# Rotary rows of the keys: a fold on TensorE for each head in the bank of its other rows, in place of one fold and a GpSimd copy

## The chip, the cores and the metric

The kernel runs on one core of a Trainium2 chip. The metric is the device time of one execution in microseconds, the median of several runs. A core has TensorE (PE in the profile, its weight loads PEld), VectorE (DVE), ScalarE (ACT), GpSimd (POOL) and SyncE (SP), which issues the loads from memory.

## What is computed

A network of two layers on 256 tokens of width 1024. Layer 0 mixes latent attention with a state-space scan (S5), layer 1 is a long convolution; each is followed by a mixture of 64 experts. All of the change lies in the keys of layer 0's attention, which the reference makes like this (cut):

```python
def mla_keys_values(part, kv_norm, w_ukv, k_qk, cos, sin):
    B, L, _ = part.shape
    c_kv = rmsnorm(part[..., :KV_LORA], kv_norm)
    kv = (c_kv @ w_ukv).reshape(B, L, MLA_HEADS, QK_NOPE + V_HEAD)
    k_r = jnp.broadcast_to(part[..., None, KV_LORA:KV_LORA + QK_ROPE], (B, L, MLA_HEADS, QK_ROPE))
    k = rmsnorm(jnp.concatenate([kv[..., :QK_NOPE], k_r], axis=-1), k_qk)
    if cos is not None:
        k = rope_tail(k, cos, sin)
    return k, kv[..., QK_NOPE:]
```

There are 8 heads. A key has 96 features: 64 of its own head (QK_NOPE) and 32 rotary ones (QK_ROPE), which are the same for all heads. They are made for 512 tokens, 256 of the sequence and 256 of the context.

## The kernel before

Everything lies in one arena of on-chip memory and in eight banks (`ps`, 128 rows x 512 f32), and each engine runs a program of its own; the order is written out by hand, and semaphores carry the dependences. `Chain.then` makes an engine wait for its own instruction. `mm` (L752) is TensorE's helper for a product, so nearly all products have that line; `f` (L1416) is ScalarE's.

The stage around the change goes as follows on TensorE. It projects the tokens: the latent of keys and values (`kvl`, bank 0), the rotary rows, the latent of the queries, and then the four parts of the S5 input (`proj_u`). Between these stand chunks of the modulation matrix (`ada_chunk`, L446: eight products with 24 columns each, four side by side in four quarters of bank 7), whose weights SyncE loads one after another, each when the one before has been used. The rotary rows have only 32 output rows, so their eight partial products are spread over the four quarters of bank 1 (group `g = k % 4`), and ScalarE copies the whole bank to `krl`. `fold` is a 128x32 matrix made of four 32x32 identities: a product with it adds up the four quarters. Before the change this product is made once (L851), into rows 64 to 95 of bank 1; ScalarE copies them to rows 64 to 95 of `krl` (L1467), and GpSimd, once all projections have been read, copies them to rows 64 to 95 of all eight heads of `kh` (L687, 32 x 4096).

After the projections come the S5 tables turned for each block (`b_piece`, L805), the queries' heads (L867 and on, 96 rows), and the keys' heads (L876 to L880): for each head a product of 64 columns of `w_ukv` with `kvl`, into rows 0 to 63 of bank `h % 3`. ScalarE evicts each to `kh[0:NOPE, h]` (L1492), and TensorE may run three heads ahead. After the eighth eviction TensorE goes on with S5 products (`estimates`, 64 columns each) and with the sums of squares of the queries' heads (`head_sum`, 32 columns each, heads in the order 0, 2, 1, 3, 4, 6, 5, 7, two in each quarter of bank 0; head 4 and later ones write rows 64 to 127). Then the values, `chunk_kernels` (L752, 32 columns), two idle products, and the scaling of the queries (`over_features`), which waits for VectorE's copies of the chunk kernels (L1854 to L1857).

VectorE meanwhile computes the S5 tables (L1790 to L1826), and between them the norms of the latents: L1838 and L1839 scale `kvl`. ScalarE squares `kh` for the norms of the keys from `square_head(4)` on, and waits for `kr_copied` before it (L1515). From there on the norms of the keys, the rotation (`rope`), the scores and the rest follow, each released by the one before; later loads of SyncE wait for `ada_used`, `ada_mm`, `y_mm`, `att_mm` and `x_mixed`, all of them signals of the computing engines.

Of the kernel before, what the change touches and what calls it, by code (L numbers as in the profile page):

```python
# [11 lines left out]
ACT = mybir.ActivationFunctionType  # L12
AX = mybir.AxisListType

P = 128
D = 1024
KD = D // P
L = 256
EPS = 1e-6
HEADS, NOPE, ROPE, VH = 8, 64, 32, 64  # L20
QKH = NOPE + ROPE
# [104 lines left out]
def program(nc, A):  # L126
# [8 lines left out]
    with ExitStack() as ctx:  # L135
        sems = {}

        def sem(name):
            if name not in sems:
                sems[name] = ctx.enter_context(nc.semaphore(name))  # L140
            return sems[name]
# [3 lines left out]
        ps = ctx.enter_context(nc.psum_tensor("ps", [P, 8, 512], F32))  # L145
# [11 lines left out]
        def at(a, width, rows=P):  # L157
            return ar[0:rows, a:a + width]
# [9 lines left out]
        def cst(name, rows=P):  # L168
            a, w = CST[name]
            return at(r_cst + a, w, rows)  # L170
# [4 lines left out]
        def tiles(a, k, n, rows=P):  # L175
            return at(a, k * n, rows).rearrange("p (k t) -> p k t", k=k)
# [27 lines left out]
        kh = tiles(ra, HEADS, 2 * L, QKH)  # L204
# [23 lines left out]
        w_ukv = at(rg + 1536, 1024)  # L228
# [3 lines left out]
        kvl, krl, ql = at(rk, 512), at(rk + 512, 512), tiles(rk + 1024, 2, L)  # L232
# [136 lines left out]
        def most_tokens(li, eng):  # L369
            return eng.value_load(flags[:, li:li + 1], min_val=0, max_val=L + HALF)  # L370

        def overflow(eng, body, most, s=1):

            with eng.If(most > s * S):
                with eng.Fori(0, NE) as i:
                    body(s, i)
                if s < L // S:
                    overflow(eng, body, most, s + 1)
            eng.nop()
# [295 lines left out]
        @block.gpsimd  # L675
        def _(pool):
            ch = Chain(pool, sem("pool_chain"), sem)
            ch.then(pool.memset(ones, 1.0), "ones_ready")
            pads = at(r_pad, 1)
            ch(pool.memset(pick2, 0.0))  # L680
            ch.then(pool.memset(pick2[:, 1:2], 1.0), "ones_ready")
            A8, B8 = tiles(tmp5, 2, NT5), tiles(tmp5 + 64, 2, NT5)
            t1, t2 = tiles(tmp5 + 128, 2, NT5), tiles(tmp5 + 192, 2, NT5)
            tt = pool.tensor_tensor
            pool.wait_ge(sem("kvl_evicted"), 4)
            pool.wait_ge(sem("proj_mm"), 8)
            ch.then(pool.tensor_copy(kh[NOPE:QKH], krl[NOPE:QKH].unsqueeze(1).broadcast_to([ROPE, HEADS, 2 * L])), "kr_copied")  # L687

            def squared(out_a, out_b, a, b):

                ch(tt(t1, a, a, ALU.mult))
                ch(tt(t2, b, b, ALU.mult))
                ch(tt(tmp_a, a, b, ALU.mult))
                ch(tt(out_b, tmp_a, tmp_a, ALU.add))
                ch(tt(out_a, t1, t2, ALU.subtract))

            def step(out, a, b, state, flipped, add, w1, w2):

                ch(tt(w1, a, state, ALU.mult))
                ch(tt(w2, b, flipped, ALU.mult))  # L700
                ch(tt(w1, w1, add, ALU.add))
                ch(tt(out, w1, w2, ALU.add))

            pool.wait_ge(sem("est_ready"), 8)
            a8, b8 = (v.unsqueeze(1).broadcast_to([P, XCH // 2, 2, NT5]) for v in (A8, B8))
            step(tree, a8, b8, est[:, 0:XCH:2], est[:, 0:XCH:2, ::-1], est[:, 1:XCH:2], wide, tree)
            squared(pair_a, pair_b, A8, B8)
            a, b, src, n = pair_a, pair_b, tree, 16
            for out in (est[:, 0:8], tree[:, 0:4], est[:, 0:2], st[:, 2:3]):
                n //= 2  # L710
                w1, w2 = wide[:, 0:n], wide[:, 8:8 + n]
                step(out, a.unsqueeze(1).broadcast_to([P, n, 2, NT5]), b.unsqueeze(1).broadcast_to([P, n, 2, NT5]),
                     src[:, 0:2 * n:2], src[:, 0:2 * n:2, ::-1], src[:, 1:2 * n:2], w1, w2)
                if n > 1:
                    squared(step_a, step_b, a, b)
                    a, b = step_a, step_b
                src = out
            pool.wait_ge(sem("combined"), 1)
            for j in range(XCH // 2 - 1):
                step(st[:, 4 + 2 * j], pair_a, pair_b, st[:, 2 + 2 * j], st[:, 2 + 2 * j, ::-1], pair_in[:, j], t1, t2)  # L720
            ch.then(pool.memset(pads, 0.0), "scan_done")

            pool.wait_ge(sem("combined"), 2)
            ch.then(pool.tensor_copy(stb, st[:, 1 + XCH:1:-1].rearrange("p s r (g d) -> p s r g d", d=2)[:, :, :, :, 1]), "scan_done")

            def moe_pool(li):
                ov_pad = at(r_pad + 1 - li, 1)

                def gather(out, index, name):
                    pool.indirect_dma_start(out, None, scr["h_scr"], bass.IndirectOffsetOnAxis(index, 0), bounds_check=L - 1,  # L730
                                            oob_is_err=False).then_inc(sem(name), 16)

                pool.wait_ge(sem("hscr_out"), 16 * (li + 1))
                pool.wait_ge(sem("tables_ready"), TABLES * (li + 1))
                pool.wait_ge(sem("tx_mm"), (li + 1) * NG)

                def more(s, i):
                    pool.wait_ge(sem(f"ov_d{li}"), i * OVD + OVD * NE * (s - 1) + OV_INDEX)
                    pool.wait_ge(sem(f"ov_t{li}"), i + NE * (s - 1) + 1)
                    pool.tensor_tensor(ov_pad, ones[:, 0:1], ones[:, 0:1], ALU.add).then_inc(sem(f"ov_t{li}"), 1)  # L740
                    gather(rows_of[0:S, 0], ib[:, 0:1], f"ov_q{li}")
                pool.memset(ov_pad, 0.0).then_inc(sem(f"ov_t{li}"), 1)  # L742
                overflow(pool, more, most_tokens(li, pool))

            moe_pool(0)
            moe_pool(1)
# [3 lines left out]
        def _(pe):  # L750
            def mm(out, lhsT, rhs, start, stop, skip=False):
                return pe.matmul(out, lhsT, rhs, start=start, stop=stop, skip_group_check=skip)  # L752
# [91 lines left out]
            def proj_u(i):  # L844
                for k in range(KD):
                    last = mm(ps[:, 3 + i, :], w_in[:, k, UOFF + i * P:UOFF + (i + 1) * P], hT[:, k], k == 0, k == KD - 1)
                last.then_inc(sem("proj_mm"), 1)
            pe.wait_ge(sem("uw_in"), 48)
            proj_u(0)
            pe.wait_ge(sem("kvl_evicted"), 2)  # L850
            mm(ps[NOPE:QKH, 1, :], cst("fold"), krl, True, True).then_inc(sem("proj_mm"), 1)  # L851
            ada_chunk(pe, FIRST + 1)
            proj_u(1)
            ada_chunk(pe, FIRST + 2)
            pe.wait_ge(sem("squared"), 4)
            pe.wait_ge(sem("kvl_evicted"), 4)
            for i in range(2):
                last = mm(ps[:, 2, 0:L], ones, sql[0][:, i * L:(i + 1) * L], i == 0, i == 1)
            last.then_inc(sem("norm_mm"), 1)
# [17 lines left out]
            for h in range(HEADS):  # L877
                if h >= 3:
                    pe.wait_ge(sem("kh_evicted"), h - 2)
                mm(ps[0:NOPE, h % 3, :], w_ukv[:, h * P:h * P + NOPE], kvl, True, True).then_inc(sem("head_mm"), 1)  # L880

            def estimates(b):
                q, r = b // 2, b % 2
# [528 lines left out]
        def _(act):  # L1412
            ch = Chain(act, sem("act_chain"), sem)

            def f(out, in_, func, **kw):
                return act.activation(out, in_, func, **kw)  # L1416
# [36 lines left out]
            ch.then(f(sql[1], kvl, ACT.Square), "squared")  # L1453

            def u_evict(i):
                act.wait_ge(sem("proj_mm"), 4 + min(i, 1) + i)
                ch.then(f(u_sb[:, i], ps[:, 3 + i, :].rearrange("p (c t) -> p t c", t=T5), ACT.Copy), "u_evicted")

            def b_evict(n):
# [3 lines left out]
                act.wait_ge(sem("bt_turned"), n + 1)  # L1463
                ch.then(f(bm[:, q % 2, 4 * hb:4 * hb + 4, r], ps[:, 1 + n % 2 if n >= 8 else 2 * (n % 2), :].rearrange("p (t m) -> p t m", t=4), ACT.Copy), "bm_evicted")
            u_evict(0)
            act.wait_ge(sem("proj_mm"), 5)
            ch.then(f(krl[NOPE:QKH], ps[NOPE:QKH, 1, :], ACT.Copy), "kvl_evicted")  # L1467
            u_evict(1)
            ch.then(rms(2, L, 2, "norm_mm", width=QL, out=rsx[:, 0:L]), "rms_ready")
            ch.then(rms(1, 512, 3, "norm_mm", width=KVL), "rms_ready")  # L1470
            u_evict(2)
            u_evict(3)
            for n in range(8):
# [15 lines left out]
                    square_head(b)  # L1489
            for h in range(HEADS):  # L1490
                act.wait_ge(sem("head_mm"), 4 + h + 1)
                ch.then(f(kh[0:NOPE, h], ps[0:NOPE, h % 3, :], ACT.Copy), "kh_evicted")  # L1492
            square_head(3)

            def est_evict(b):
# [16 lines left out]
                ch.then(f(vt[:, t], ps[:, 3 + t, :], ACT.Copy), "vt_evicted")  # L1512
            est_evict(2)
            est_evict(3)
            act.wait_ge(sem("kr_copied"), 1)  # L1515
            for n in range(4, 7):
                square_head(n)
            for n in range(8, 12):
# [913 lines left out]
```

## Time and profile before

| | us |
|---|---|
| median of 3 runs (lowest, highest) | 1443.02 (1441.14, 1443.29) |
| profiled execution, its own time | 1447.34 |
| its span | 1445.5 |
| TensorE busy in the span | 1303.6 (90%) |
| VectorE busy | 639.0 (44%) |
| ScalarE busy | 300.4 (21%) |
| GpSimd busy | 60.2 (4%) |
| mean rate of the DMA queues | 348 GB/s |

The profile is of one execution. The span is the time from the first to the last instruction; the profiled execution's own time is 1.8 us longer. A product in f32 stands in the trace as two instructions (passes) with a weight load each. Ends of matmuls are modelled, so their starts are the surer number; a weight load without "idle before" was loaded while a product ran, and one with idle time started only when the engine got to it. A line of the chain of work tells on what the end depended at that time.

### The profile page before, as it was taken

To read this page: it belongs to the slowest core of one execution; us is meant where nothing else is said; L and a number is where in the kernel's file an instruction comes from. 1 tells how busy PE (TensorE), PEld (TensorE's weight loads), DVE (VectorE), ACT (ScalarE), POOL (GpSimd) and SP (SyncE) were. 2 spreads that over 40 slices of the span, in tenths; PEclk is the share of its full clock that TensorE was granted. 3 is DMA by queue.
4 is the path that set the end of the run, shared out by engine and by line. 5 is a ranking of instruction groups with operands and counts; after the bars stand their busy time and mean duration, and the time that the engine had idled before them with its cause. 6 is when DMAs were issued, how large, how long until landed. Compare 5 with 4: busy or idle time off the path is not lost.

```text
span 1445.5 us, 21852 instructions
## 1 busy us (share of the span) xinstructions
PE 1303.6 (90%) x9044; PEld 678.7 (47%) x9044; DVE 639.0 (44%) x1175; ACT 300.4 (21%) x508; POOL 60.2 (4%) x112
## 2 busy tenths in 40 slices
PE   5999888999999978889888999999999978888888
PEld 1445335764444433334345676874454434333334
DVE  5998862254433222232233678864433323222232
ACT  2226342311111111111112113131111111111111
POOL 0000680000000000000000000000000000000000
PEclk9999999899999999999999999999999999999999
DMA  9673874959999999999998772587999999999995
GB/s 374 244 200 83 164 240 183 412 226 371 421 425 420 426 430 429 427 430 427 427 422 294 292 284 117 206 361 303 374 426 421 422 430 425 429 428 427 428 425 241
DMA packets 52598, 502.76 MB, mean 348 GB/s; under 512 B 9548, under 2 KB 16460, under 8 KB 20044
## 3 DMA queue, kind: packets, MB, share of 16 engines
q1 hardware_dynamic: 51948, 499.18, 86.0%
q10 hardware_dynamic: 544, 2.10, 0.4%
q8 instruction: 75, 1.23, 0.3%
q14 instruction: 31, 0.25, 0.1%
HBM read 496.57 MB, written 4.69 MB: 347 GB/s over the span
## 4 chain that ended last, share of the span: by engine, by line
PE 59%; DMA 28%; DVE 8%; issue 2%; SPq 1%; ACT 1%; DVEq 0%; ACTq 0%
PE ps L752 55%; DMA arena<-in_w_experts 23%; DMA arena<-in_ada_w 4%; PE ps L1070 2%; PE ps L446 2%; SPq L490 1%; DVE arena L2049 1%; ACT arena L1416 1%; DVE arena L2150 0%; DVE arena L1876 0%; PE ps L805 0%; DVE arena L1871 0%; DVE arena L1872 0%; DVE arena L1889 0%; PE ps L1017 0%
## 5 line engine op out<-in xcount | busy, mean ns | idle before, releaser
L752 PE MATMUL ps<-arena 128*32 128x512 f32 (+10 forms) x8224 | 1219.9, 485 | 122.0 <-issue 48.6
L752 PEld LDWEIGHTS ps<-arena 128*32 128x32 f32 (+5 forms) x8224 | 616.9, 130 | 709.9 <-issue 586.9
L1416 ACT ACTIVATE arena<-ps 128x512 f32<-128x512 f32 (+6 forms) x305 | 168.5, 552 | 926.2 <-PE ps L752 767.5
L1416 ACT ACTIVATE arena<-arena 128x256 f32<-128x256 f32 (+7 forms) x143 | 94.5, 682 | 153.2 <-DVE arena L2110 58.3
L2090 DVE SCALAR_TENSOR_TENSOR arena<-arena,ps 128x256 f32<-128x256 f32 x44 | 21.1, 480 | 233.7 <-ACT arena L1416 233.7
L2108 DVE CAST arena<-ps 128x512 bf16<-128x512 f32 x42 | 29.1, 692 | 165.2 <-PE ps L752 165.2
L2045 DVE COPY arena<-ps 128x512 f32<-128x512 f32 x44 | 30.4, 692 | 126.9 <-PE ps L752 126.9
L2078 DVE TENSOR_TENSOR arena<-arena 128x1024 bf16<-128x1024 f32 x42 | 51.5, 1225 | 37.3 <-ACT arena L1416 37.0
L1070 PE MATMUL ps<-arena 128*128 128x128 f32 x352 | 52.8, 273 | 0.0
L2110 DVE TENSOR_TENSOR arena<-ps,arena 128x1024 f32<-128x1024 f32 x42 | 51.4, 1224 | 1.4
L742 POOL MEMSET arena<- 128x1 f32 x2 | 0.2, 102 | 1192.3 <-PE ps L1070 1192.3
L2049 DVE COPY arena<-ps 128x512 f32<-128x512 f32 x44 | 30.4, 692 | 26.3 <-PE ps L1070 26.3
L1070 PEld LDWEIGHTS ps<-arena 128*128 128x128 f32 x352 | 41.4, 141 | 0.0
L446 PE MATMUL ps<-arena 128*24 128x512 f32 x256 | 34.6, 637 | 5.7 <-DMA arena<-in_ada_w 5.7
L2098 DVE COPY arena<-ps 128x256 f32<-128x256 f32 x44 | 18.6, 422 | 31.0 <-PE ps L1070 31.0
L1416 ACT ACTIVATE arena<-ps,arena 128x512 f32<-128x512 f32 (+3 forms) x29 | 17.0, 585 | 35.9 <-DVE arena L1890 20.4
L1416 ACT ACT_TABLE_LOAD x15 | 19.2, 1283 | 22.0 <-PE ps L752 9.9
L2242 DVE SCALAR_TENSOR_TENSOR arena<-arena 128x512 f32<-128x512 f32 x28 | 21.1, 752 | 1.1 <-DMA arena<-in_ada_w 0.2
L1017 PE MATMUL ps<-arena 128*128 128x128 f32 x64 | 10.9, 297 | 8.1 <-DVE arena L1895 8.0
L446 PEld LDWEIGHTS ps<-arena 128*24 128x24 f32 x256 | 6.3, 103 | 24.5 <-issue 16.6
L1017 PEld LDWEIGHTS ps<-arena 128*128 128x128 f32 x64 | 7.8, 149 | 18.8 <-DVE arena L1895 15.5
L2086 DVE TENSOR_SCALAR arena<-arena 128x256 bf16<-128x256 f32 (+1 forms) x44 | 15.3, 347 | 0.1
(234 smaller groups left out, 481.1 us busy)
## 6 DMA issues: line engine op xcount, KB each, us to landing
arena<-in_w_experts SPq DMA_DIRECT2D x76, 3072.0 KB, 20.8
arena<-in_w_experts SPq DMA_DIRECT2D x80, 1024.0 KB, 11.6
arena<-in_w_experts SPq DMA_DIRECT2D x38, 2048.0 KB, 19.8
arena<-in_ada_w SPq DMA_DIRECT2D x40, 1024.0 KB, 6.6
arena<-in_hy_w_in SPq DMA_DIRECT2D x6, 2048.0 KB, 11.1
arena<-in_ada_w SPq DMA_DIRECT2D x4, 2048.0 KB, 22.9
arena<-in_w_shared SPq DMA_DIRECT2D x2, 3072.0 KB, 10.1
arena<-in_hy_w_out SPq DMA_DIRECT2D x1, 4096.0 KB, 12.1
```

The lines of the kernel that those rows point to most:

```text
L446: last = pe.matmul(ps[32 * k:32 * k + 2 * GROUP, 7, :], scz[:, 4 * half + k, a:a + 2 * GROUP], ada_half(i, half)[:, k], start=i == first a ...
L752: return pe.matmul(out, lhsT, rhs, start=start, stop=stop, skip_group_check=skip)
L1017: last = pe.transpose(ps[:, 2 + n % 2, k * P:(k + 1) * P], prob[:, n % 3, k * P:(k + 1) * P], ident)
L1070: return mm(out, in_, one, True, True) if first else pe.transpose(out, in_, one)
L1416: return act.activation(out, in_, func, **kw)
L2045: dve.tensor_copy(picked[:, 512:], ps[:, DN + 1, :]).then_inc(sem("picked_dve"), 1)
L2049: dve.tensor_copy(xgT[:, 4:8].rearrange("p k t -> p (k t)"), ps[:, DN + 1, :]).then_inc(sem("xt_dve"), 1)
L2078: tt(yb[:, 2], yr, yb[:, 1], SU).then_inc(sem("y_dve"), 1)
L2090: stt(hh, sg, wtab[:, n:n + 1], ps[:, GU, FF:2 * FF], M, M).then_inc(sem("h_done"), 1)
L2108: ch(dve.tensor_copy(yb[:, 0, 0:512], ps[:, DN, :]))
L2110: tt(yr, ps[:, DN:DN + 2, :].rearrange("p b n -> p (b n)"), yb[:, 0], SU).then_inc(sem("y_dve"), 1)
L2242: ins = ts(ada_sums[n], w, c, None, M) if half == 0 and k == 0 else stt(ada_sums[n], w, c, ada_sums[n], M, AD)
```

## The change

The product with `fold` is made for each head, into rows 64 to 95 of the same bank as the head's own 64 rows and right behind it; the eviction of a head then copies 96 rows. The single fold, its eviction and the copy on GpSimd are left out, and so are the waits for them; `krl` keeps the four quarters. Counts of `proj_mm` and `kvl_evicted` shrink by the instruction that is gone.

```diff
@@ -682,9 +682,6 @@
             A8, B8 = tiles(tmp5, 2, NT5), tiles(tmp5 + 64, 2, NT5)
             t1, t2 = tiles(tmp5 + 128, 2, NT5), tiles(tmp5 + 192, 2, NT5)
             tt = pool.tensor_tensor
-            pool.wait_ge(sem("kvl_evicted"), 4)
-            pool.wait_ge(sem("proj_mm"), 8)
-            ch.then(pool.tensor_copy(kh[NOPE:QKH], krl[NOPE:QKH].unsqueeze(1).broadcast_to([ROPE, HEADS, 2 * L])), "kr_copied")
 
             def squared(out_a, out_b, a, b):
 
@@ -847,13 +844,11 @@
                 last.then_inc(sem("proj_mm"), 1)
             pe.wait_ge(sem("uw_in"), 48)
             proj_u(0)
-            pe.wait_ge(sem("kvl_evicted"), 2)
-            mm(ps[NOPE:QKH, 1, :], cst("fold"), krl, True, True).then_inc(sem("proj_mm"), 1)
             ada_chunk(pe, FIRST + 1)
             proj_u(1)
             ada_chunk(pe, FIRST + 2)
             pe.wait_ge(sem("squared"), 4)
-            pe.wait_ge(sem("kvl_evicted"), 4)
+            pe.wait_ge(sem("kvl_evicted"), 3)
             for i in range(2):
                 last = mm(ps[:, 2, 0:L], ones, sql[0][:, i * L:(i + 1) * L], i == 0, i == 1)
             last.then_inc(sem("norm_mm"), 1)
@@ -877,7 +872,8 @@
             for h in range(HEADS):
                 if h >= 3:
                     pe.wait_ge(sem("kh_evicted"), h - 2)
-                mm(ps[0:NOPE, h % 3, :], w_ukv[:, h * P:h * P + NOPE], kvl, True, True).then_inc(sem("head_mm"), 1)
+                mm(ps[0:NOPE, h % 3, :], w_ukv[:, h * P:h * P + NOPE], kvl, True, True)
+                mm(ps[NOPE:QKH, h % 3, :], cst("fold"), krl, True, True).then_inc(sem("head_mm"), 1)
 
             def estimates(b):
                 q, r = b // 2, b % 2
@@ -1453,7 +1449,7 @@
             ch.then(f(sql[1], kvl, ACT.Square), "squared")
 
             def u_evict(i):
-                act.wait_ge(sem("proj_mm"), 4 + min(i, 1) + i)
+                act.wait_ge(sem("proj_mm"), 4 + i)
                 ch.then(f(u_sb[:, i], ps[:, 3 + i, :].rearrange("p (c t) -> p t c", t=T5), ACT.Copy), "u_evicted")
 
             def b_evict(n):
@@ -1463,8 +1459,6 @@
                 act.wait_ge(sem("bt_turned"), n + 1)
                 ch.then(f(bm[:, q % 2, 4 * hb:4 * hb + 4, r], ps[:, 1 + n % 2 if n >= 8 else 2 * (n % 2), :].rearrange("p (t m) -> p t m", t=4), ACT.Copy), "bm_evicted")
             u_evict(0)
-            act.wait_ge(sem("proj_mm"), 5)
-            ch.then(f(krl[NOPE:QKH], ps[NOPE:QKH, 1, :], ACT.Copy), "kvl_evicted")
             u_evict(1)
             ch.then(rms(2, L, 2, "norm_mm", width=QL, out=rsx[:, 0:L]), "rms_ready")
             ch.then(rms(1, 512, 3, "norm_mm", width=KVL), "rms_ready")
@@ -1489,7 +1483,7 @@
                     square_head(b)
             for h in range(HEADS):
                 act.wait_ge(sem("head_mm"), 4 + h + 1)
-                ch.then(f(kh[0:NOPE, h], ps[0:NOPE, h % 3, :], ACT.Copy), "kh_evicted")
+                ch.then(f(kh[:, h], ps[0:QKH, h % 3, :], ACT.Copy), "kh_evicted")
             square_head(3)
 
             def est_evict(b):
@@ -1512,7 +1506,6 @@
                 ch.then(f(vt[:, t], ps[:, 3 + t, :], ACT.Copy), "vt_evicted")
             est_evict(2)
             est_evict(3)
-            act.wait_ge(sem("kr_copied"), 1)
             for n in range(4, 7):
                 square_head(n)
             for n in range(8, 12):
```

## Rows read from the trace of the kernel before

**Rows 1.** The page: the span, and its chain by engine.

```profile
span 1445.5 us, 21852 instructions
...
PE 59%; DMA 28%; DVE 8%; issue 2%; SPq 1%; ACT 1%; DVEq 0%; ACTq 0%
```

**Rows 2.** The chain of work in order of time: start us, us, what. The front.

```profile
103.32 13.95 PE ps L752 x48
...
118.09 8.03 PE ps L752 x120
...
128.39 3.68 PE ps L752 x128
132.07 0.43 DVE arena L1854
...
134.66 1.12 PE ps L752 x16
```

**Rows 3.** The same chain, later.

```profile
143.14 3.37 DVE arena L1864
...
206.35 7.26 DMA arena<-in_ada_w
```

**Rows 4.** Timeline 57 to 105 us: start, us, engine, line, op, shapes, count [idle <-releaser].

```profile
66.60 0.11 PEld L752 LDWEIGHTS ps<-arena 128*32 128x32 f32 x1 [0.76 <-issue]
...
66.60 0.63 PE L446 MATMUL ps<-arena 128*24 128x512 f32 x3
...
69.29 0.30 PEld L752 LDWEIGHTS ps<-arena 128*128 128x128 f32 x2 [0.84 <-issue]
...
76.37 0.14 PEld L446 LDWEIGHTS ps<-arena 128*24 128x24 f32 x8 [0.76 <-issue]
...
78.22 1.16 PEld L752 LDWEIGHTS ps<-arena 128*128 128x128 f32 x6 [0.84 <-issue]
```

**Rows 5.** One load of modulation weights: issue, and time to landing.

```profile
L490 SPq DMA_DIRECT2D arena<-in_ada_w x1: 328/328/328, 59.6 to 59.6; - x1
...
DMA to landing us min/median/max: 6.6/6.6/6.6
```

**Rows 6.** Timeline, weight loads of TensorE at the heads of the keys.

```profile
110.17 0.19 PEld L752 LDWEIGHTS ps<-arena 128*64 128x64 f32 x2 [0.36 <-issue]
110.65 0.14 PEld L752 LDWEIGHTS ps<-arena 128*64 128x64 f32 x1 [0.29 <-issue]
111.08 0.13 PEld L752 LDWEIGHTS ps<-arena 128*64 128x64 f32 x1 [0.29 <-issue]
```

**Rows 7.** Timeline, evictions by ScalarE: the last of the queries, the second of the keys.

```profile
110.34 0.59 ACT L1416 ACTIVATE arena<-ps 96x512 f32<-96x512 f32 x1 [0.47 <-PE ps L752]
...
112.20 0.59 ACT L1416 ACTIVATE arena<-ps 64x512 f32<-64x512 f32 x1 [0.27 <-PE ps L752]
```

**Rows 8.** L752 by shape, 119.7 to 120.18 us: ns min/median/max, first and last start.

```profile
L752 PE MATMUL ps<-arena x12: 377/380/380, 119.4 to 119.9; 96*32 96x256 f32 x12
```

**Rows 9.** Timeline, the weight loads that come next.

```profile
120.19 0.19 PEld L752 LDWEIGHTS ps<-arena 128*64 128x64 f32 x3 [0.41 <-issue]
```

**Rows 10.** Timeline, the GpSimd copy and VectorE around it.

```profile
93.28 0.48 DVE L1836 SCALAR_TENSOR_TENSOR arena<-arena 128x256 f32<-128x256 f32 x1
...
96.19 3.60 POOL L687 COPY arena<-arena 32x4096 f32<-32x4096 f32 x1 [94.94 <-PE ps L752]
...
97.19 3.16 DVE L1839 SCALAR_TENSOR_TENSOR arena<-arena 128x512 f32<-128x512 f32 x1
```

**Rows 11.** Timeline, what ends ahead of the step at 134.66 us.

```profile
130.28 1.75 DVE L1849 RECIPROCAL arena<-arena 128x256 f32<-128x256 f32 x1
...
132.47 1.88 PE L752 MATMUL ps<-arena 128*128 128x512 f32 x4
```

**Rows 12.** Stretches: PE, PEld, DVE, ACT, POOL busy (count), granted clock, DMA share, GB/s.

```profile
110.00:118.00 8.00, 7.26 (x18) 2.09 (x16) 7.66 (x11) 5.35 (x10) 0.00 (x0) 1.00 0.40 26
...
160.00:168.00 8.00, 7.69 (x20) 2.48 (x24) 3.13 (x6) 0.00 (x0) 7.53 (x7) 0.59 0.84 73
```

## Prediction

> **What bounds the kernel now.** I read the page first: one core, a span of 1445.5 us, and a chain of work that is TensorE for 59% and DMA for 28% [rows 1]. The change touches only the first attention stage, so the question is which engine ends last there, and whether a shift made there survives to the end. The chain in order of time answers the first. From 59 us to 103 us it is TensorE alone (the projections, the modulation chunks, the turned tables); from 103.32 to 117.3 us it is the heads, 13.95 us of L752 in one piece, the queries' heads first and then the eight key heads; ScalarE's last eviction leads to 118.09 (the first estimates), and that to 128.39 (the chunk kernels), to VectorE's copies at 132.07 and back to TensorE at 134.66 [rows 2]. From 143.14 on VectorE carries it, first with the reciprocal of the keys' norms [rows 3]. So the key heads stand on the path: each microsecond added to them is one added to all that follows, unless something later was waiting for another thing anyway.
>
> Does it survive? At 206.35 the chain runs for 7.26 us through loads of modulation weights [rows 3]. They look like an absolute clock, but aren't: by the code, SyncE issues each of them only when TensorE has used the chunk before, so they move with TensorE. The same holds for the expert loads (they wait for y_mm, x_mixed and tables_ready). Between the heads' start and the chunk kernels' end SyncE issues no load at all. A shift at 118 us is therefore a shift at the end.
>
> **The change part by part.** All in the profiled execution's time.
>
> *The early fold goes.* It is two passes (a matmul in f32 is two instructions, each streaming all its columns). The fold starts at 66.60 beside three products of the modulation chunk, and the next projection starts at 69.29: 2.69 us. The same chunk without a fold takes 78.22 - 76.37 = 1.85 us [rows 4]. The fold costs 0.84 us, since its 32 rows of the output are also a quarter of the chunk's. The chain stays on TensorE from there to the turned tables, so this comes back whole: **-0.84**. The chunk's last weights were issued at 59.6 and took 6.6 us to land [rows 5], so they are there before 66.60 and don't take the gain. The eviction of the folded rows (32x512 on ScalarE) waits for TensorE anyway and is worth nothing.
>
> *Eight folds come, one behind each head's product.* The price hangs on one thing: does a product of 32 columns run beside one of 64? They write disjoint rows of the bank (0 to 63 and 64 to 95), and the early fold shows that products in disjoint rows can run side by side: it started together with three others [rows 4]. But all four were at most 32 columns wide. A head's product is 64 wide [rows 6]. Does the trace show a 64 and a 32 beside each other? It shows them behind each other, which tells as much. The queries' head sums (32 columns, 256 streamed) start their last passes at 119.9 us [rows 8]; by the program these are heads 4 to 7, which write rows 64 to 127. Next in the queue is a product of 64 columns into rows 0 to 63 of another bank, with all its waits met. Nothing overlaps it, and yet its weights are loaded only at 120.19, with 0.41 us of idle before [rows 9]: 256 columns at the measured pace (0.43 us per 512 [rows 6]) are 0.21, so it came after the streaming of the sums plus nearly 0.1 us. Within one width a weight load goes ahead of the running product (two at 110.17 [rows 6]); here it did not. So the width of the tile is a mode, and changing it empties the engine.
>
> I take it that each fold runs after its head's product, and the next product after the fold. The terms: a pass is 0.43 us (110.65 to 111.08), so a fold is 0.86. A change into the narrow width costs what the modulation chunk of rows 4 shows over its four rounds: 1.85 - 4 x 0.43 = 0.13 us, one entry and one exit shared. A change into the 64-wide: the first pass took 110.65 - 110.17 = 0.48 in place of 0.43 [rows 6], and emptying adds the 0.1 above, so 0.15. Sum: 8 x (0.86 + 0.13) = 7.92, and 7 returns x 0.15 = 1.05: **+9.0**. The bounds: nothing at all below (all folds hidden beside the heads), and 8 x (0.86 + 0.20) + 7 x 0.20 = 9.9 above, with 0.20 from the 128-wide projection (76.37 - 69.29 = 7.08 for 16 passes of 0.43 [rows 4]). I take 9.0, which is nearest to the rows of these very widths. A head then takes some 2.0 us where it took 0.86 (ScalarE's evictions keep that step with 0.27 us of idle [rows 7]).
>
> The Trainium skill, page "TensorEngine Tiling (Array Packing)", section "Tiling Modes", says that changing the tiling mode, not just the tile, drains TensorE, and lists 128x64 and 128x32 as different modes; by that rule the folds cost the whole sum, and rows 8 and 9 agree with it. The Trainium skill's page "TensorE: Matmul & The Clock Gate", section "Why this matters for your kernels", says that products with few output columns in distinct column groups run together; read alone, it would price the folds at nothing, which is the first rival below, and rows 4 agree with it for one width.
>
> *Eviction of 96 rows for 64.* A 96x512 copy from the bank took 0.59 us, a 64x512 one 0.59 [rows 7]: **0**. ScalarE has over 1 us of idle per head in the new step, and the three banks in rotation are freed in time.
>
> *The GpSimd copy goes.* It ran 96.19 to 99.79 us. VectorE's L1839, 128x512, started at 97.19 and took 3.16 us, to 100.35: it ended 0.56 us after the copy did; L1836, half as wide, took 0.48 [rows 10]. So L1839 waited for the copy, and VectorE comes out about 2.4 us earlier. Is that on the path? Only at 132.07, where its first copy (L1854) starts right after its own reciprocal ended at 132.03 [rows 11] although the first half of the chunk kernels was done well before. But the next step on TensorE (134.66) stands behind two idle products, which run from 132.47 for 1.88 us, to 134.35 [rows 11]. Freed earlier, VectorE could do half of its copies before 132.07, about 1.2 us of them, but the gain shrinks to 134.66 - 134.35: **-0.3**. The same 0.3 comes if TensorE is late and VectorE isn't, so it doesn't hang on the copy. ScalarE's removed wait (kr_copied) had long been met, and the changed counts of proj_mm and kvl_evicted ask for the same work as before: 0.
>
> **Sum:** -0.84 + 9.0 + 0 - 0.3 = **+7.8 us**. What becomes late next is everything on TensorE behind the heads, with the same slack as before; VectorE and ScalarE wait the longer. On the profiled execution, 1445.5 us become 1453.3. On the median of the runs, 1443.02, it is **1450.8 us**. The profiled execution took 1447.34 with what lies around its span, 4.3 above that median, and I carry the difference over, not the level.
>
> **The rivals.**
> *A, the folds are hidden* (the other side). If 64 and 32 columns run side by side, a head stays at 0.86 us, and only the gains are left: -0.84 - 0.3 = -1.1, 1441.9 us. For it: disjoint rows, and the four side by side in rows 4. Against it: rows 8 and 9, where disjoint rows didn't help once the width changed. It decides if the second product of a head starts less than about 0.2 us behind the first. I give it 0.11.
> *B, half hidden.* If a fold can start beside its head's second pass, but the next head must wait for it, each adds 0.86 + 0.13 - 0.43 = 0.56 us, 4.5 in all, and 1443.02 + 4.5 - 1.1 is 1446.4. Nothing in rows 8 and 9 looks like it. 0.06.
> *C, the clock.* In the 8 us from 160 us the granted clock was 0.59 of full speed, where the eight passes of the key rotation run at half pace; in the heads' stretch it was 1.00 [rows 12]. Moved by some 8 us, such a dip can fall on less or on more work: the eight passes cost 8 x 0.43 = 3.4 us more at the low level (1.2 GHz for 2.4), so up to -3.4 or +3.4 from there: 1447.4 to 1454.2. It isn't a different cause, but widens the forecast. It gets 0.10, half on each side.
> The forecast itself has 0.73.
>
> **How the numbers follow.** The likeliest case gives 1450.8. Its own range, from the terms' bounds and the spread of the runs (1441.14 to 1443.29), is 1448.8 to 1452.5. With most of C and part of B it is 1446.5 to 1453.8, which leaves out A, the lower part of B and the tails. A measurement of this kernel can tell about 0.2%, 2.9 us, from no change. A at 1441.9 is within that, except where other small gains join it: faster 0.02, within 0.11, slower 0.87.
>
> **What the new profile should show.** At the key heads ScalarE's evictions about 2.0 us apart, with a 32-wide weight load between each pair of 64-wide ones and each first load of a new width without lead; the last eviction some 8 us later than 117.4. The stretch from the first u projection to the next one shorter by 0.84 us. L1839 at 0.7 us, no POOL copy. VectorE idle before the chunk kernels' copies. The distance from the first estimates to the first scores unchanged, save for the 0.3. It would be wrong if the evictions stay 0.86 us apart (A), or if they spread but the score stage starts less than 5 us later (B).

## The result and the profile after

The changed kernel is slower: 1449.23 us median of 17 runs (1444.18 to 1451.64) against 1442.27 us for the kernel before on the same chip (17 runs, 1439.53 to 1448.28). The ratio is 1.0034 with a 95% interval of 1.0025 to 1.0043, that is +4.9 us (3.6 to 6.2). The medians lie 7.0 us apart and the means 5.5, because the runs of before scatter in two heaps, around 1441 and 1447, and the profiled execution of before came from the upper one. The profiled execution of after (1446.34 us, span 1444.4) came from the low end of its own runs. So the two spans can't be set against each other; their stretches can. The forecast was 1450.8 us, with +7.8 for the change.

The page of after, its first lines and its chain:

```profile
span 1444.4 us, 21876 instructions
...
PE 62%; DMA 27%; DVE 7%; issue 2%; SPq 1%; ACT 1%; DVEq 0%; ACTq 0%
```

The chain of after in order of time (start us, us, what), beside rows 2:

```profile
58.39 7.08 PE ps L749 x16
65.47 1.85 PE ps L446 x16
67.32 7.08 PE ps L749 x16
...
101.26 22.78 PE ps L749 x64
...
124.86 8.03 PE ps L749 x120
...
135.15 3.64 PE ps L749 x128
...
139.38 2.77 PE ps L749 x20
```

L749 is `mm`, L752 before. The projection at 58.39 stood at 59.59 in before (startup took 1.2 us less in this execution). From it to the first estimates are 66.47 us, against 58.50: **+7.97**, where 8.16 was forecast. The heads' piece is 22.78 us for 13.95, +8.83. The modulation chunk without its fold takes 1.85 us, as forecast from 2.69. The idle products and the scaling of the queries run through (139.38, x20) with no copy of VectorE between them.

The timeline of after, weight loads on TensorE in the heads of the keys, beside rows 6:

```profile
109.12 0.14 PEld L749 LDWEIGHTS ps<-arena 128*32 128x32 f32 x2 [0.81 <-issue]
110.09 0.19 PEld L749 LDWEIGHTS ps<-arena 128*64 128x64 f32 x2 [0.84 <-issue]
111.09 0.14 PEld L749 LDWEIGHTS ps<-arena 128*32 128x32 f32 x2 [0.81 <-issue]
112.07 0.19 PEld L749 LDWEIGHTS ps<-arena 128*64 128x64 f32 x2 [0.84 <-issue]
```

Widths alternate, and not one load of a new width starts while a product of the other runs: two passes, then the next width, 0.97 to 1.00 us each. ScalarE's evictions (96 rows, still 0.59 us) stand 1.98 us apart, with 1.39 us of idle where rows 7 show 0.27:

```profile
110.26 0.59 ACT L1412 ACTIVATE arena<-ps 96x512 f32<-96x512 f32 x1 [1.39 <-PE ps L749]
112.24 0.59 ACT L1412 ACTIVATE arena<-ps 96x512 f32<-96x512 f32 x1 [1.39 <-PE ps L749]
```

### The profile page after: what moved, and what is told of

Same layout as the page of the kernel before. It is cut to its first block, busy times and chain, and to the rows that moved or that the text cites. A ratio compares the mean times of both kernels' runs of the same rounds, so it can differ in the third digit from the quotient of the medians.

```text
span 1444.4 us, 21876 instructions
## 1 busy us (share of the span) xinstructions
PE 1304.5 (90%) x9058; PEld 674.6 (47%) x9058; DVE 637.2 (44%) x1175; ACT 299.9 (21%) x507; POOL 56.5 (4%) x111
## 4 chain that ended last, share of the span: by engine, by line
PE 62%; DMA 27%; DVE 7%; issue 2%; SPq 1%; ACT 1%; DVEq 0%; ACTq 0%
PE ps L749 57%; DMA arena<-in_w_experts 23%; DMA arena<-in_ada_w 4%; PE ps L1066 2%; PE ps L446 2%; DVE arena L2042 1%; SPq L490 1%; ACT arena L1412 1%; DVE arena L1869 0%; DVE arena L2235 0%; PE ps L802 0%; DVE arena L1882 0%; DVE arena L1745 0%; PE ps L1013 0%; DVE arena L1888 0%
## 5 line engine op out<-in xcount | busy, mean ns | idle before, releaser
L749 PE MATMUL ps<-arena 128*32 128x512 f32 (+10 forms) x8238 | 1221.6, 484 | 122.4 <-issue 48.0
L749 PEld LDWEIGHTS ps<-arena 128*32 128x32 f32 (+5 forms) x8238 | 612.5, 130 | 715.4 <-issue 587.5
L1412 ACT ACTIVATE arena<-ps 128x512 f32<-128x512 f32 (+4 forms) x304 | 167.9, 552 | 929.8 <-PE ps L749 773.0
L696 POOL TENSOR_TENSOR arena<-arena 128x64 f32<-128x64 f32 (+4 forms) x20 | 10.0, 500 | 163.6 <-ACT arena L1412 162.1
```

## The experiments

Times are medians; each ratio is to the kernel before on the same chip. Differences along the way come from the profiled executions.

### The changed kernel again

No edit.

> The changed kernel once more, as the yardstick of the others on the same chip. Theory W (a change between the 64-wide and the 32-wide tile empties TensorE): 8.1 us later at the first estimates than the kernel before, counted from the first modulation chunk after the projections, and 5 to 8 us longer in all, since the low-clock stretches fall differently. Rival N (the profiled gap was chance): no difference.

Measured: 1449.29 us against 1442.59, ratio 1.0039 (1.0024 to 1.0054). The stretch from SyncE's first load of modulation weights after 57 us to the load behind the chunk kernels is 7.97 us longer than in before, against 7.96 in the first profile. N (the profiled gap was chance) falls.

### Three products of the same width

```diff
-mm(ps[0:NOPE, h % 3, :], w_ukv[:, h * P:h * P + NOPE], kvl, True, True)
+for half in range(2):
+    c = h * P + half * ROPE
+    mm(ps[half * ROPE:(half + 1) * ROPE, h % 3, :], w_ukv[:, c:c + ROPE], kvl, True, True)
 mm(ps[NOPE:QKH, h % 3, :], cst("fold"), krl, True, True).then_inc(sem("head_mm"), 1)
```

> Each head's 64-wide product is cut into two 32-wide ones, so that all three products of a head have the same width and disjoint rows; same result, 24 products in place of 16. Theory W: the three run side by side, evictions 0.86 us apart, the first estimates 8.9 us earlier than in the changed kernel and 0.8 us earlier than before; in all 1 us faster than before, which is within what can be told. Rival S (what costs is a second moving operand, krl beside kvl, or a third product on the bank): evictions 1.7 us apart or more, as slow as the changed kernel or slower.

Measured: 1437.22 us, ratio 0.9952 (0.9935 to 0.9969). The heads take 13.96 us, as if there were no folds. The timeline's weight loads of this kernel, three to a load step, 0.43 us apart:

```profile
108.61 0.15 PEld L749 LDWEIGHTS ps<-arena 128*32 128x32 f32 x6 [0.36 <-issue]
109.07 0.12 PEld L749 LDWEIGHTS ps<-arena 128*32 128x32 f32 x3 [0.31 <-issue]
109.50 0.12 PEld L749 LDWEIGHTS ps<-arena 128*32 128x32 f32 x3 [0.31 <-issue]
```

W holds and S falls: neither the second moving operand nor a third product costs anything. The place and the size there are as expected; the whole gained 4 to 6 us more than W's 1 us, which opened the question of the later experiments.

### The fold as wide as the head

```diff
-mm(ps[NOPE:QKH, h % 3, :], cst("fold"), krl, True, True).then_inc(sem("head_mm"), 1)
+mm(ps[NOPE:P, h % 3, :], at(r_cst + CST["fold"][0], NOPE), krl, True, True).then_inc(sem("head_mm"), 1)
```

> The fold is made 64 wide (32 more columns of the neighbouring constants, whose rows 96 to 127 of the bank nobody reads), so that both products of a head have the width 64. Theory W: they run side by side, evictions 0.86 us apart, in all as split32. Rival Q (only 32-wide products can run beside one another): evictions 1.72 us apart, 6.9 us slower than before at the first estimates.

Measured: 1440.79 us, ratio 0.9982 (0.9969 to 0.9995). The heads take 13.97 us; the loads come in pairs:

```profile
110.11 0.14 PEld L749 LDWEIGHTS ps<-arena 128*64 128x64 f32 x2 [0.29 <-issue]
110.55 0.14 PEld L749 LDWEIGHTS ps<-arena 128*64 128x64 f32 x2 [0.29 <-issue]
110.97 0.14 PEld L749 LDWEIGHTS ps<-arena 128*64 128x64 f32 x2 [0.29 <-issue]
```

Twice the columns for the same fold, and the 8.83 us are gone. So it is the inequality of widths that costs, not narrowness. Q falls. One part of the expectation missed: in all this kernel is 3.6 us slower than the one with three 32-wide products, where W had them alike. In the first profiles of the two a difference of 3.7 us arises between 152 and 229 us, far behind the heads.

### The order turned for every second head

```diff
-mm(ps[0:NOPE, h % 3, :], w_ukv[:, h * P:h * P + NOPE], kvl, True, True)
-mm(ps[NOPE:QKH, h % 3, :], cst("fold"), krl, True, True).then_inc(sem("head_mm"), 1)
+own = lambda: mm(ps[0:NOPE, h % 3, :], w_ukv[:, h * P:h * P + NOPE], kvl, True, True)
+rotary = lambda: mm(ps[NOPE:QKH, h % 3, :], cst("fold"), krl, True, True)
+for product in (own, rotary) if h % 2 == 0 else (rotary, own):
+    last = product()
+last.then_inc(sem("head_mm"), 1)
```

> The changed kernel with the order of a head's two products turned round for every second head (own, fold, fold, own, own, fold, ...), so that the width changes 8 times in place of 15; the passes are the same 32. Theory W prices a change at 0.12 to 0.15 us of emptying and a slower first pass: the first estimates 7 x 0.12 to 0.15 = 0.8 to 1.0 us earlier than in the changed kernel. If the emptying were most of the cost (rival V), they would come 4 us earlier or more.

Measured: 1448.20 us, ratio 1.0030 (1.0015 to 1.0046). The chain of this kernel has the heads at

```profile
101.96 21.88 PE ps L749 x64
```

which is 0.90 us less than 22.78 for 7 changes fewer: 0.13 us a change. V falls. Of the 8.83 us, 15 changes are 1.9 and the folds' own 16 passes of 0.43 are 6.9: most of the price is that a fold can't hide, not the emptying itself. The first estimates come only 0.50 us earlier than in the changed kernel: 0.40 us was lost ahead of the heads, where in this execution a modulation chunk waited for its weights.

### A plain delay on TensorE

```diff
 pe.wait_ge(sem("kh_evicted"), HEADS)
+idle_products(1, 9)
 estimates(0)
```

> The kernel before with nine idle 128-wide products of 512 columns (18 passes) after the last key head, 18 x 0.43 + 0.2 = 7.9 us of TensorE and nothing else. If a delay on TensorE at this place is all that the change does, the whole time rises as in the changed kernel (theory W). If it survives whole, 7.9 us; if the low-clock stretches and a later wait take part of it, 4 to 7 us in both kernels alike. Rival P (the changed kernel has another cost, or the removal of the GpSimd copy gives more than 0.3 us): the two differ by over 2 us.

Measured: 1448.76 us, ratio 1.0035 (1.0020 to 1.0049), the changed kernel's numbers. At the load behind the chunk kernels it is 7.88 us late, the changed kernel 7.96. P falls: in the whole time the change can't be told from that delay. And the delay, like the change, loses some of it on the way to the end: by the ratio 5.0 us (2.9 to 7.1) arrive.

### Only the removals

```diff
-mm(ps[0:NOPE, h % 3, :], w_ukv[:, h * P:h * P + NOPE], kvl, True, True)
-mm(ps[NOPE:QKH, h % 3, :], cst("fold"), krl, True, True).then_inc(sem("head_mm"), 1)
+mm(ps[0:NOPE, h % 3, :], w_ukv[:, h * P:h * P + NOPE], kvl, True, True).then_inc(sem("head_mm"), 1)
-ch.then(f(kh[:, h], ps[0:QKH, h % 3, :], ACT.Copy), "kh_evicted")
+ch.then(f(kh[0:NOPE, h], ps[0:NOPE, h % 3, :], ACT.Copy), "kh_evicted")
```

> The changed kernel without the eight folds, and with evictions of 64 rows: the rotary rows of the keys are left out (they hold what was there). What is left of the change is the removal of the early fold and of the GpSimd copy. Theory W: 0.84 us earlier at the first estimates, 1.1 us at the scaling of the queries, in all 1441 to 1443. Rival G (the copy's removal is worth more than VectorE's row shows, by its earlier tables): over 3 us faster than before.

Measured: 1443.08 us, ratio 1.0002 (0.9989 to 1.0016). Locally it is 0.84 us early behind the heads and 0.39 us more after the scaling of the queries, just the forecast's terms; G falls. But hardly any of it reaches the end. At the first VectorE step of the experts (309.03 us in before) 0.35 of the 1.23 us are left, since a stall in TensorE's S5 outputs grew by 0.86 us. It is a wait in the middle of products without a semaphore, for which the profile names no releaser. Timeline, PE: first this kernel, then before, then after:

```profile
235.68 10.59 PE L749 MATMUL ps<-arena 64*32 64x128 f32 x162 [2.41 <-issue]
```

```profile
239.07 7.13 PE L752 MATMUL ps<-arena 64*32 64x128 f32 x112 [1.55 <-issue]
```

```profile
242.37 3.93 PE L749 MATMUL ps<-arena 64*32 64x128 f32 x85 [0.24 <-issue]
```

### Only the cut, and the cut kernel again

```diff
-mm(ps[0:NOPE, h % 3, :], w_ukv[:, h * P:h * P + NOPE], kvl, True, True).then_inc(sem("head_mm"), 1)
+for half in range(2):
+    c = h * P + half * ROPE
+    last = mm(ps[half * ROPE:(half + 1) * ROPE, h % 3, :], w_ukv[:, c:c + ROPE], kvl, True, True)
+last.then_inc(sem("head_mm"), 1)
```

> The kernel before, with each key head's 64-wide product cut into two 32-wide ones, no fold added, nothing removed. On TensorE it takes the same time as before. The cut kernel with folds was 6 us faster than before where its own steps explain 1.1. If that surplus comes from cutting the products (8 more instructions with their weight loads in TensorE's program, another place where its code is fetched, another fall of the low-clock stretches), this kernel is 3 to 5 us faster than before too; if it was chance or belongs to the removals, it is within 1.5 us of before.

> The kernel with the cut products once more. If its 1437.2 holds, 1436 to 1438.5; if part of it was chance, 1440 to 1442, as its own steps say.

Measured: 1440.42 us, ratio 0.9983 (0.9970 to 0.9997), for the cut alone, between the expectation's two cases, and 1437.65 us, ratio 0.9967 (0.9950 to 0.9983), for the cut with folds, again, as expected if the first 1437.22 holds. In the cut-only kernel the stretch to behind the chunk kernels is within 0.02 us of before, so its 2.8 us come later. Its stall in the S5 outputs is 0.25 us.

### Eight idle products

```diff
+pe.wait_ge(sem("kh_evicted"), HEADS - 1)
+for _ in range(8):
+    mm(ps[:, 0, 0:8], ident, at(r_cst, 8), True, True)
 pe.wait_ge(sem("kh_evicted"), HEADS)
 estimates(0)
```

The same lines were put into the kernel before and into the one with only the removals.

> The kernel before, with eight idle products of 8 columns on TensorE while it waits for the last key eviction (some 0.5 us of work inside a wait of 0.83 us, so nothing on the path). Theory L (where the rest of TensorE's program lies in the stream of its instructions decides the length of a stall that has no releaser, 1.5 us in the S5 outputs of the kernel before and about 0.3 us in every version with more products): the stall is 0.2 to 0.4 us and the whole time 2 to 3 us lower, 1440 to 1441.5, as in the kernel that only cuts the products. Rival M (the cut itself, side-by-side 32-wide products, gave that kernel its 2.8 us): no change from before.

> The kernel without the folds (the rotary rows of the keys are left out), with the same eight idle products. Theory L: it loses its 2.4 us stall and then shows what the two removals are worth, 1.2 us less than the padded kernel before: 1439 to 1440.5. Rival M: 1443, as without them.

Measured: 1440.34 us, ratio 0.9985 (0.9973 to 0.9998), for the padded kernel before: useless work makes it faster, by 2.2 us (0.3 to 3.9). The cover was misjudged: the products cost 1.00 us on the path. M falls, and L holds where it arises: the S5 stall is there, but short, and the stretch from 229 to 315 us is 2.5 us shorter:

```profile
237.37 8.87 PE L752 MATMUL ps<-arena 64*32 64x128 f32 x155 [0.23 <-issue]
```

The padded removals: 1441.16 us, ratio 0.9992 (0.9984 to 1.0001). The stall is gone and behind the chunk kernels it is 0.86 us ahead of the padded before, but its whole time is not; this was a miss of L's 1.2 us, and differences of that size aren't resolved by whole times here.

### Twice the delay, and before again

```diff
+idle_products(1, 18)
```

> The kernel before with 18 idle products (36 passes, 15.5 us) after the last key head. If a delay on TensorE survives whole and only a fixed 2.4 us comes back through the shorter stalls of a longer program (theory L): 15.7 - 0.4 - 2.4 = 12.9 us, 1455 to 1457. If a share of it is absorbed on the way (rival A2, a third, as the first delay of 7.9 us became 5.3): 10.5 us, 1453 to 1454.

> The kernel before, profiled once more. Theory L: its stall of about 1.5 us in the S5 outputs is there again. The 3.5 us by which its first profile is longer than all others between 782 and 837 us, where TensorE's clock fell at 801 us, are chance and are gone; if they are there again, the longer versions gained them lastingly.

Measured: 1454.54 us, ratio 1.0091 (1.0073 to 1.0108), +13.1 us (10.5 to 15.6). It stands 15.58 us late behind the chunk kernels. The centre of the interval is near L's 12.9 and A2's 10.5 lies at its edge, but the median of the six runs, 1454.54, falls between L's 1455 to 1457 and A2's 1453 to 1454, so the whole time doesn't decide. The stretch from 229 to 315 us says more: it gives back 1.9 us here and 2.6 after the shorter delay, so the loss there doesn't grow with the delay. The stall is 0.69 us, longer than L's 0.2 to 0.4. Before again: 1442.34 us, ratio 1.0003 (0.9992 to 1.0014). Its stall is 1.98 us. The surplus around 801 us is partly there again. From 801 to 837 us the first profile of before is 3.3 us longer than eleven other profiles, this one 2.6 us, the padded before 1.7 us, and only these three have a fall of the clock at 801 to 804 us. The padded before has more products and shows it, the removals have fewer and don't: so it isn't a gain of the longer versions, and what sets it stays open.

## Why the prediction was right, and where it wasn't

**The width as a mode: right.** Rows 8 and 9 carried it, one place in the trace where disjoint rows didn't help once the width changed. Three kernels show it from both sides: unequal 22.78 us, all 32 wide 13.96, all 64 wide 13.97. The Trainium skill's page "TensorEngine Tiling (Array Packing)", section "Tiling Modes", says that a change of mode drains the engine, and these runs agree with it. Rival A is out, and B with it (evictions 1.98 us apart, where B wanted about 1.4).

**The terms.** Folds: forecast 9.0, measured 8.83. The small miss is the price of a change, 0.13 us from the reordered kernel where 0.13 and 0.15 were taken. Early fold: forecast -0.84, measured -0.84 (the removals alone). Eviction of 96 rows: 0, measured 0.59 us as before.

**The GpSimd copy: right in size, less sure in cause.** In after, L1839 (now L1832) takes 0.75 us and the 0.39 us are gained, 0.3 having been forecast. But look at before again, timeline of VectorE and GpSimd:

```profile
96.91 0.75 DVE L1839 SCALAR_TENSOR_TENSOR arena<-arena 128x512 f32<-128x512 f32 x1
97.23 3.88 POOL L687 COPY arena<-arena 32x4096 f32<-32x4096 f32 x1 [95.98 <-PE ps L752]
```

The same program, and here VectorE came first: its operation took 0.75 us, and the 0.38 us were gained with the copy in place. Which of the two starts first depends on a few tenths of a microsecond, so this 0.3 is a term of the execution I read (rows 10), not of the kernel. The second profile of the cut kernel with folds shows it from the other side: no copy, 0.75 us for the operation, and yet VectorE's copies of the chunk kernels (129.28 to 131.72 us) end last and the scaling is 0.12 us later than in before, counted from the first estimates, since TensorE had started its projections earlier beside VectorE.

**"A shift at 118 us is therefore a shift at the end": the step that was too strong.** Of 7.8 us some 5 arrived: by the ratio 4.9 (3.6 to 6.2), and 7.8 lies above that interval. That the level came out only 1.6 us from the forecast 1450.8 is in part luck: the difference of the medians, 7.0 us, is the largest of the three ways to take it, and 1443.02 with 4.9 would be 1447.9, in the wide range (1446.5 to 1453.8) but below the likeliest case's own (1448.8 to 1452.5). Locally the sum stands: +7.97 and -0.39 by 152 us are 7.58. The reason given for its survival had a slip too: between the heads' start and the chunk kernels' end SyncE does issue loads (of `u_scr`, eight from 101.1 to 105.6 us), but no run shows that this mattered.

Two things later give back 2.4 us, and they do so, 1.9 to 3.1 us, in every version that has more products on TensorE than before:

| | S5 stall, us | clock, 275 to 300 us | stretch 229 to 315 us against before |
|---|---|---|---|
| before, before again | 1.55, 1.98 | 0.80, 0.80 | 0, +0.4 |
| removals | 2.41 | 0.80 | +2.4 |
| padded removals | none | 0.86 | -2.6 |
| after, after again | 0.24, 0.32 | 0.86, 0.86 | -2.4, -2.5 |
| idle products (9), padded before | none, 0.23 | 0.86, 0.86 | -2.6, -2.5 |
| cut only, fold 64 wide | 0.25, 0.23 | 0.86, 0.86 | -2.3, -2.5 |
| cut with folds, again | none, 0.35 | 0.86, 0.89 | -3.1, -2.3 |
| order turned | 0.40 | 0.86 | -2.4 |
| idle products (18) | 0.69 | 0.86 | -1.9 |

Of the removals' +2.4 only 0.86 us are stall; the rest is a fall of the clock at 236.8 us (3.4 us at 1.2 GHz); before's fall stands at 221 us, ahead of this stretch.

The stretches of before, the padded before and after (columns as in rows 12), in this order; 0.80 and 0.86 is the granted clock:

```profile
275.00:300.00 25.00, 22.16 (x123) 19.22 (x122) 14.01 (x50) 9.18 (x20) 0.00 (x0) 0.80 0.96 384
```

```profile
275.00:300.00 25.00, 21.99 (x131) 18.44 (x130) 15.74 (x58) 10.88 (x22) 0.00 (x0) 0.86 0.91 364
```

```profile
275.00:300.00 25.00, 21.50 (x127) 17.80 (x126) 12.76 (x43) 9.73 (x22) 0.00 (x0) 0.86 0.98 393
```

For the change as made about 1.3 us are the shorter stall, 1.1 us a shorter low-clock stretch behind it (10.2 us at 1.2 GHz in the three with the long stall, at most 6.8 in the others). Together: 7.58 - 2.4 = 5.2, inside the measured 3.6 to 6.2. That is an account of the part that repeats; between 152 and 229 us the two profiles of the changed kernel differ by 3.4 us from each other (1.6 less and 1.8 more than before), so a single profile carries chance as large as what is explained here. That more instructions bring the shorter stall is shown by the padded kernel, which computes nothing new, and by the cut-only kernel, which comes there without any delay (0.02 us).

The traces say what kind of wait it is. In all eleven profiles with a stall of 0.23 us or more it stands behind the same number of instructions, 1349 passes, and not at the same product of the program. These are the stretches from the start to the middle of the stall, PE and PEld first (columns as in rows 12), in before, after and the kernel with 18 idle products, whose programs have 0, 14 and 36 more passes ahead of it:

```profile
0.00:238.50 238.50, 201.10 (x1349) 94.36 (x1350) 176.13 (x282) 87.73 (x157) 59.98 (x110) 0.96 0.70 220
```

```profile
0.00:242.30 242.30, 206.04 (x1349) 93.67 (x1350) 174.02 (x282) 87.10 (x156) 56.26 (x109) 0.96 0.70 217
```

```profile
0.00:250.00 250.00, 213.57 (x1349) 100.02 (x1350) 176.77 (x282) 87.58 (x157) 59.65 (x110) 0.97 0.67 210
```

Each time it ends 1.4 to 1.6 us after one packet of the queue that the profile calls instruction, which moves 16 KB packets (the page of before, then the packets of that queue between 236.5 and 238 us, where before's stall is):

```profile
q8 instruction: 75, 1.23, 0.3%
```

```profile
q8 instruction: 1, 0.02, 4.0%
```

In before that packet starts at 236.76 us, when TensorE is 0.8 us from the 1349 passes' end; in after it starts at 239.99, 2.1 us ahead of it; in the removals only with it. The fixed count and the packet together say that TensorE waits there for its own code, and that the stall is short where the packet starts early enough; this is read from the traces, and no run delayed the packet by itself. What makes it start earlier with more products ahead isn't shown, nor whether the stall makes the clock's stretch longer or only goes with it.

**Rival C** was on the list as a widening of the range, and this is half of what happened. It had the size of a fall (3.4 us) but took it as chance of either sign; here the part at 279 us came with one sign in all profiles.

**The level.** I carried the difference to the median (1443.02 + 7.8), not the span. With a profiled execution 4.3 us above the median, that mattered: rows 1 set against after's page show 1.1 us *less*, for a kernel that is slower.

**A faster version.** The cut kernel with folds (three 32-wide products to a head) gave 1437.22 and 1437.65 us: 5 to 7 us under before and 12 under the change as it was made, and leaves nothing of the computation out. Its steps explain 0.84 + 0.39 + 2.4 = 3.6 us at most (the 0.39 only in its first profile). The rest arises in both of its profiles between 152 and 229 us, 2.0 and 2.5 us less than before there, where the 64-wide fold has 1.8 more. TensorE's clock stayed whole between 215 and 235 us in both (1.00, where before and the 64-wide fold show 0.83), but that isn't the explanation by itself: the cut-only kernel has 1.00 there too and gains 0.1 us in that stretch. So the surplus is measured twice in the whole time, and its cause is open.

## What to carry to other kernels

Products on TensorE that are to run side by side must have the same tile width (64 and 32 columns did not run together here, the 24 and 32 of rows 4 did): give the narrow one dead columns or cut the wide one, and look in the trace for weight loads in groups with no idle longer than a pass ahead of them. Ahead of a forecast, mark which of its rows would differ in another execution of the same program: who of two engines starts first, a stall without a releaser, a fall of the clock. A shift that is whole where it arises still has to pass those, and an edit of a few instructions can move them as much as it moves its own place.

## What the runs showed of the hardware that I had not expected

Eight idle products made the kernel faster (1440.34 for 1442.73, by the ratio 2.2 us, 0.3 to 3.9), although they cost 1.00 us where they stand: TensorE's wait with no named releaser in the middle of the S5 outputs fell from between 1.55 and 2.41 us to at most 0.40 us in the versions with 14 to 30 more passes (0.69 with 36), and stayed in every version without. Wherever it is seen it stands behind 1349 passes, whatever they compute, and it ends 1.4 to 1.6 us after a packet of the instruction queue.

A GpSimd copy and a VectorE operation held each other up in whichever order they came: the copy first, VectorE's 128x512 operation took 3.16 us in place of 0.75 (rows 10); VectorE first, the copy took 3.88 us in place of 3.60 (and 4.06 in the kernel with nine idle products, where the two overlapped longer).
